# The two FFN layers of a streaming encoder: from plain tile products to Strassen's seven half-size products, with the hidden layer in three chunks

## The chip, the cores and the metric

One core of one Trainium2 chip runs the whole program in one launch. The metric is the device time of that launch in microseconds (us), as the median of several runs. Lower is better.

## What is computed

`x` is 512 tokens by 1024 features, float32. Two layers follow each other: an S5 state-space mixer and then a retention mixer, each followed by a SwiGLU FFN of width 2816, with an RMS norm ahead of each of the four and one at the end. The change touches the FFN alone:

```
def rmsnorm(x, g):
    y = x * lax.rsqrt(jnp.mean(jnp.square(x), axis=-1, keepdims=True) + 1e-6)
    return y * g
def swiglu(u, w_gate, w_up, w_down):                 # u: 512 x 1024
    h = jax.nn.silu(u @ w_gate) * (u @ w_up)         # w_gate, w_up: 1024 x 2816
    return h @ w_down                                # w_down: 2816 x 1024
x = x + swiglu(rmsnorm(x, ffn_norm[i]), ...)         # i = 0, 1
```

## The kernel before

Everything is kept transposed: features lie on the 128 partitions, the 512 tokens in the free dimension. `xT` is 8 such tiles, and the hidden layer is 22 (`FT`). Each float32 operand is split into a high part, rounded to the type float32r, and the remainder as a low part (`u_hi`, `u_lo`; `w_hi`, `w_lo`). `product` issues three matmuls for a 128 x 128 block of weights: high by high, high by low, low by high, each with 512 moving columns. The RMS norm's factor per token (`rs`) is applied to what comes out of the matmuls.

Weights arrive in units of up to 1 MB in two slots (`s` = 0 and 1). For each unit SyncE's queue loads `w_raw[s]`, ScalarE makes `w_hi[s]`, VectorE makes `w_lo[s]` by a subtraction (`split_weights`, once on each engine), and TensorE uses them; semaphores (`w_loaded`, `w_hi_ready`, `w_lo_ready`, `w_used`) count the pairs of units. Every engine runs its own instructions strictly in the order written; nothing is scheduled by a tool.

An FFN layer is a loop of 11 rounds. In a round, slot 0 holds 256 columns of the gate weights and slot 1 the same of the up weights, for two hidden tiles; each unit is 48 matmuls (2 tiles x 8 blocks x 3). VectorE takes the gate out of PSUM times `rs` (line 1544), ScalarE applies silu (line 1119), VectorE takes the up part out times `rs` and multiplies the two (line 1203), ScalarE makes `h_hi`, VectorE `h_lo` (line 1558). All 22 tiles of the hidden layer stay in SBUF. Then come the 8 output tiles: each is 22 blocks x 3 = 66 matmuls into one PSUM bank, and VectorE adds it to `xT` (line 1470), with the next norm's input and squares made right behind. A layer is 22 x 48 + 8 x 66 = 1584 matmuls of 512 columns.

Of the kernel before, what the change touches and what calls it, by code (L numbers as in the profile page):

```python
# [20 lines left out]

# [6 lines left out]
F32 = mybir.dt.float32  # L28
# [5 lines left out]
P = 128  # L34
# [23 lines left out]
PAIRS = {"glu": 2, "ffn0": 11, "down0": 8, "ret": 12, "wo": 4, "ffn1": 11, "down1": 8}  # L58
# [58 lines left out]
def bank_starts():  # L117
# [34 lines left out]
FREE0, FULL0 = bank_starts()  # L152

# [9 lines left out]
def trunk(nc, x, s5_norm, lam_re, lam_im, log_step, b_re, b_im, c_re, c_im, s5_d, glu_w, glu_b,  # L163
          ret_norm, ret_w, ret_gn, ret_wo, ffn_norm, ffn_gate, ffn_up, ffn_down, final_norm,
          ident_in, rope_in, decay_in, out):
    with ExitStack() as ctx:
# [105 lines left out]
        last.close()  # L272
        u_hi = sb(ctx, "u_hi", [P, KT, SEQ], F32R)
# [4 lines left out]
        y_whole = tmp[:, 6, :]  # L278
        sq = tmp[:, 4, :]
# [7 lines left out]
        ffn = ExitStack()  # L287
        h_hi = sb(ffn, "h_hi", [P, FT, SEQ], F32R)
        h_lo = sb(ffn, "h_lo", [P, FT, SEQ], F32R)
        ffn.close()  # L290
# [82 lines left out]
        w_used = [sem(f"w_used{s}") for s in range(2)]  # L373

# [43 lines left out]


# [28 lines left out]
        def _(sp):  # L448
# [62 lines left out]
            def ffn_units(layer):  # L511
                with sp.Fori(0, HT) as i:
                    load_unit(0, i + PAIR0[f"ffn{layer}"], gate_v[layer][:, :, bass.ds(i * 256, 256)], KT, 256)
                    load_unit(1, i + PAIR0[f"ffn{layer}"], up_v[layer][:, :, bass.ds(i * 256, 256)], KT, 256)
                with sp.Fori(0, KT) as i:
                    for s in range(2):
                        load_unit(s, i + PAIR0[f"down{layer}"],
                                  down_v[layer][:, HT * s:HT * s + HT, bass.ds(i * P, P)], HT, P)

            ffn_units(0)  # L520
# [15 lines left out]
            ffn_units(1)  # L536
# [8 lines left out]
        def _(pe):  # L545
# [222 lines left out]
            def rms_sum(norm):  # L768

                b0 = FREE0[f"norm{norm}"][7]  # L770
                pe.wait_ge(sum_done, (KT + 1) * (norm + 1))
                open_bank(7, b0)
                pe.matmul(bank[7][:, :], ones[:, :], sq_sum, start=True, stop=True).then_inc(bank_full[7], 1)
# [14 lines left out]
            def ffn_products(layer, norm):  # L788
                def hidden_tiles(i, s, split):

                    banks = [2 * s, 2 * s + 1]
                    two_tiles(s, i + PAIR0[f"ffn{layer}"], banks, [i + FREE0[f"ffn{layer}"][b] for b in banks],
                              split, KT * norm)

                hidden_tiles(0, 0, u_split)
                rms_sum(norm)
                hidden_tiles(0, 1, None)
                with pe.Fori(1, HT) as i:
                    for s in range(2):
                        hidden_tiles(i, s, None)  # L800
                with pe.Fori(0, KT // 2) as i:
                    for m in range(2):
                        b = 4 + m
                        open_bank(b, i + FREE0[f"down{layer}"][b])
                        for s in range(2):
                            pe.wait_ge(w_lo_ready[s], i * 2 + PAIR0[f"down{layer}"] + m + 1)
                            for k in range(HT):
                                kk = HT * s + k
                                pe.wait_ge(h_split, FT * layer + kk + 1)
                                mm = product(bank[b][:, :], s, slice(P * k, P * k + P), h_hi[:, kk, :],  # L810
                                             h_lo[:, kk, :], kk == 0, kk == FT - 1)
                            mm.then_inc(w_used[s], 1)

            ffn_products(0, 0)
# [75 lines left out]
            ffn_products(1, 2)  # L890
# [30 lines left out]
        def _(act):  # L921
# [150 lines left out]
            def root(i):  # L1072

                b = FULL0[f"norm{i}"][7]
                act.wait_ge(bank_full[7], b + 1)
                act.activation(rs, bank[7][:, :], ACT.Sqrt, bias=eps[:, :], scale=1.0 / D).then_inc(bank_free[7], 1)
# [5 lines left out]


            for t in range(KT):
# [7 lines left out]
                if t in GLU_SPLIT_AT:  # L1092
                    split_weights(m // 2, i + PAIR0["glu"] + 1)
                act.wait_ge(x_new, t + 1)
                u_high(0, t, V_FFN0)
                square(t)
            root(0)

            def ffn(layer, i_norm, gain_col):
                def body(i, last_of_all):  # L1100

                    for m in range(2):
                        pair = i * 2 + m + PAIR0[f"down{layer}"]
                        if not (last_of_all and m == 1):
                            split_weights(0, pair + 1)
                        if last_of_all and m == 1:
                            act.activation(small[:, 27:28], eps[:, :], ACT.Sqrt)
                        act.wait_ge(bank_free[4 + m], i + FREE0[f"down{layer}"][4 + m] + 1)
                        if i_norm < 3:
                            u_high(i_norm, i * 2 + m, gain_col)  # L1110
                        square(i * 2 + m)
                        if not (last_of_all and m == 1):
                            split_weights(1, pair + 1)

                with act.Fori(0, HT) as i:
                    pair = i + PAIR0[f"ffn{layer}"]
                    for m in range(2):
                        act.wait_ge(bank_free[m], i + FREE0[f"ffn{layer}"][m] + 1)
                        act.activation(sig[:, m, :], sig[:, m, :], ACT.Silu).then_inc(gate_ready, 1)  # L1119
                    split_weights(0, pair + 1)  # L1120
                    split_weights(1, pair + 1)
                    for m in range(2):
                        act.wait_ge(h_raw_ready, i * 2 + (FT * layer + m + 1))
                        copy(tile(h_hi, i * 2 + m), act_raw[:, m, :]).then_inc(h_hi_ready, 1)
                if layer == 0:
                    with act.Fori(0, KT // 2) as i:
                        body(i, False)
                else:
                    with act.Fori(0, KT // 2 - 1) as i:
                        body(i, False)  # L1130
                    body(KT // 2 - 1, True)

            ffn(0, 1, V_RET)
# [40 lines left out]
            with act.Fori(0, KT // 2) as i:  # L1174
                for s in range(2):
                    act.wait_ge(bank_free[2 + s], i + FREE0["wo"][2 + s] + 1)
                    u_high(2, i * 2 + s, V_FFN1)
                    square(i * 2 + s)
                    split_weights(s, i + PAIR0["wo"] + 1)
            root(2)  # L1180
            ffn(1, 3, V_FINAL)
# [9 lines left out]
        def _(dve):  # L1191
# [293 lines left out]
            def inverse_rms(i):  # L1485
                dve.wait_ge(bank_free[7], FREE0[f"norm{i}"][7] + 1)
# [7 lines left out]


# [20 lines left out]
            inverse_rms(0)  # L1516

            def ffn(layer, i_norm, gain_col):
                def body(i, last_of_all):

                    for m in range(2):
                        pair = i * 2 + m + PAIR0[f"down{layer}"]
                        if not (last_of_all and m == 1):
                            split_weights(0, pair + 1)
                        dve.wait_ge(w_used[1], pair + 1)
                        add_to_x(i * 2 + m, bank[4 + m][:, :]).then_inc(bank_free[4 + m], 1)
                        dve.wait_ge(bank_free[4 + m], i + (FREE0[f"down{layer}"][4 + m] + 1))
# [317 lines left out]
```

## Time and profile before

| | |
|---|---|
| median of 3 runs | 1275.46 us (1275.38 to 1276.29) |
| span of the profiled execution, first to last instruction | 1274.6 us |
| the times shown, less that span | 0.8 to 1.7 us |
| TensorE busy, of the span | 97% |
| VectorE, ScalarE, GpSimd busy | 53%, 36%, 5% |
| second FFN layer behind its norm's sum (1536 matmuls) | 348.2 us |

The profile gives no other time of the profiled execution than its span; what lies around it is the third row. Engines overlap, so the busy shares add up to more than one, and a share says nothing of which wait ends last. TensorE's rows come as matmuls (PE) and weight loads (PEld). The duration of a matmul's row reaches over the start of the next, so the pace of TensorE is read from starts.

### The profile page before, as it was taken

How to read it: one execution, taken by the hardware profiler on the slowest of the kernel's cores; microseconds unless marked ns; L12 is line 12 of the kernel's file. 1: busy time of each engine (PE TensorE's matmuls, PEld its weight loads, DVE VectorE, ACT ScalarE, POOL GpSimd, SP SyncE). 2: the span in 40 equal slices, each digit the busy share in tenths (PEclk: the TensorE clock that was granted, in tenths of full speed). 3: DMA queues.
4: the chain of work that ended last, by engine and by line, in shares of the span. 5: the costliest groups of instructions: out<-in, count | busy, mean ns of one | idle time of the engine just before them, and what ended most of it. 6: DMA issues, size and time to landing. Idle time of an engine off the chain costs nothing.

```text
span 1274.6 us, 16378 instructions
## 1 busy us (share of the span) xinstructions
PE 1240.5 (97%) x6469; PEld 1031.8 (81%) x6469; DVE 671.5 (53%) x771; ACT 463.7 (36%) x493; POOL 64.5 (5%) x84
## 2 busy tenths in 40 slices
PE   3899999999999999999999999999999999999997
PEld 3778888888888888888888888888888888888886
DVE  8997754443444444646655465643454444444443
ACT  6555443233333333333343333422333333332232
POOL 5940000000000000000000000000000000000000
PEclk9999999999999999999999999999999999999999
DMA  5663333333323334323232133233232323323331
GB/s 116 153 123 100 99 100 99 99 99 99 99 68 90 92 91 138 108 66 108 67 99 94 45 107 99 66 99 98 67 124 77 102 92 99 99 68 91 95 109 66
DMA packets 143376, 121.31 MB, mean 95 GB/s; under 512 B 5528, under 2 KB 135632, under 8 KB 143312
## 3 DMA queue, kind: packets, MB, share of 16 engines
q1 hardware_dynamic: 141680, 118.23, 30.3%
q10 hardware_dynamic: 1664, 2.62, 1.0%
q8 instruction: 23, 0.38, 0.1%
q14 instruction: 9, 0.07, 0.0%
HBM read 114.29 MB, written 2.10 MB: 91 GB/s over the span
## 4 chain that ended last, share of the span: by engine, by line
PE 93%; POOL 3%; DVE 1%; ACTq 1%; ACT 1%; DMA 0%; issue 0%; SPq 0%; DVEq 0%; POOLq 0%
PE bank L738 27%; PE bank L740 27%; PE bank L739 27%; PE bank L836 2%; PE bank L837 2%; PE bank L838 2%; ACTq L443 1%; PE bank L865 1%; PE bank L866 1%; PE bank L864 1%; PE bank L634 1%; PE bank L875 1%; POOL s_pool_tmp L1699 1%; POOL s_seg_tmp L1699 0%; ACT w_raw L929 0%; PE bank L849 0%
## 5 line engine op out<-in xcount | busy, mean ns | idle before, releaser
L738 PE MATMUL bank<-u_hi,w_hi 128*128 128x512 f32 x960 | 374.9, 390 | 0.0
L740 PE MATMUL bank<-u_hi,w_lo 128*128 128x512 f32 x960 | 373.6, 389 | 0.0
L739 PE MATMUL bank<-u_lo,w_hi 128*128 128x512 f32 x960 | 373.5, 389 | 0.0
L1213 DVE TENSOR_TENSOR w_lo<-w_raw,w_hi 128x2048 fp32r<-128x2048 f32 x112 | 256.5, 2291 | 167.0 <-ACT w_hi L929 166.9
L929 ACT ACTIVATE w_hi<-w_raw 128x2048 fp32r<-128x2048 f32 x112 | 214.0, 1911 | 318.3 <-PE bank L740 314.9
L738 PEld LDWEIGHTS bank<-u_hi,w_hi 128*128 128x128 f32 x960 | 180.2, 188 | 37.9 <-issue 0.6
L739 PEld LDWEIGHTS bank<-u_lo,w_hi 128*128 128x128 f32 x960 | 180.2, 188 | 37.5 <-issue 0.5
L740 PEld LDWEIGHTS bank<-u_hi,w_lo 128*128 128x128 f32 x960 | 180.2, 188 | 37.4
L738 PE MATMUL bank<-h_hi,w_hi 128*128 128x512 f32 x352 | 136.9, 389 | 0.0
L739 PE MATMUL bank<-h_lo,w_hi 128*128 128x512 f32 x352 | 136.9, 389 | 0.0
L740 PE MATMUL bank<-h_hi,w_lo 128*128 128x512 f32 x352 | 136.9, 389 | 0.0
L1203 DVE TENSOR_TENSOR tmp<-bank,tmp 128x512 f32<-128x512 f32 (+3 forms) x60 | 38.1, 635 | 97.0 <-PE bank L740 94.2
L1119 ACT ACTIVATE tmp<-tmp 128x512 f32<-128x512 f32 x44 | 27.8, 632 | 136.6 <-DVE tmp L1544 135.6
L1544 DVE TENSOR_TENSOR tmp<-bank,tmp 128x512 f32<-128x512 f32 x44 | 30.0, 691 | 89.7 <-PE bank L740 89.2
L740 PEld LDWEIGHTS bank<-h_hi,w_lo 128*128 128x128 f32 x352 | 66.1, 188 | 13.8
L739 PEld LDWEIGHTS bank<-h_lo,w_hi 128*128 128x128 f32 x352 | 66.1, 188 | 13.7
L738 PEld LDWEIGHTS bank<-h_hi,w_hi 128*128 128x128 f32 x352 | 66.1, 188 | 13.7
L1470 DVE TENSOR_TENSOR xT<-bank,xT 128x512 f32 (+1 forms) x24 | 16.6, 692 | 92.5 <-PE bank L740 92.5
L1069 ACT ACTIVATE u_hi<-xT,vecs (+1 forms) x24 | 17.3, 721 | 124.4 <-DVE xT L1470 124.4
L738 PE MATMUL bank<-y_hi,w_hi 128*128 128x512 f32 x128 | 49.9, 390 | 0.0
L739 PE MATMUL bank<-y_lo,w_hi 128*128 128x512 f32 x128 | 49.8, 389 | 0.0
L740 PE MATMUL bank<-y_hi,w_lo 128*128 128x512 f32 x128 | 49.8, 389 | 0.0
(230 smaller groups left out, 1320.1 us busy)
## 6 DMA issues: line engine op xcount, KB each, us to landing
w_raw<-in_ret_w_qkvg_dram SPq DMA_DIRECT2D x24, 1024.0 KB, 5.0
w_raw<-in_ffn_w_gate_dram SPq DMA_DIRECT2D x22, 1024.0 KB, 5.1
w_raw<-in_ffn_w_up_dram SPq DMA_DIRECT2D x22, 1024.0 KB, 5.1
w_raw<-in_ffn_w_down_dram SPq DMA_DIRECT2D x32, 704.0 KB, 4.2
w_raw<-in_ret_w_o_dram SPq DMA_DIRECT2D x8, 1024.0 KB, 5.1
w_raw<-in_s_glu_w_dram SPq DMA_DIRECT2D x4, 1024.0 KB, 4.8
s<-in_x_dram ACTq DMA_DIRECT2D x8, 256.0 KB, 7.9
s_w<-in_x_dram SPq DMA_DIRECT2D x1, 2048.0 KB, 8.9
```

Source lines behind the costliest of these rows:

```text
L738: pe.matmul(o, w_hi[w][:, w_cols], hi, start=first, stop=False)
L739: pe.matmul(o, w_hi[w][:, w_cols], lo, start=False, stop=False)
L740: return pe.matmul(o, w_lo[w][:, w_cols], hi, start=False, stop=end)
L836: pe.matmul(o, a_hi, w_hi[s][:, cols], start=(kk == 0), stop=False)
L837: pe.matmul(o, a_hi, w_lo[s][:, cols], start=False, stop=False)
L838: mm = pe.matmul(o, a_lo, w_hi[s][:, cols], start=False, stop=(kk == KT - 1))
L929: return act.activation(o, i, ACT.Copy, scale=scale)
L1069: act.activation(tile(u_hi, t), tile(xT, t), ACT.Copy, scale=vecs[:, bass.ds(t + gain_col, 1)]).then_inc(u_hi_ready, 1)
L1119: act.activation(sig[:, m, :], sig[:, m, :], ACT.Silu).then_inc(gate_ready, 1)
L1203: return dve.tensor_tensor(o, a, b, ALU.mult)
L1213: dve.tensor_tensor(w_lo[s][:, :], w_raw[:, s, :], w_hi[s][:, :].bitcast(F32), ALU.subtract).then_inc(w_lo_ready[s], 1)
L1544: dve.tensor_tensor(sig[:, m, :], bank[m][:, :], rs, ALU.mult).then_inc(bank_free[m], 1)
```

## The change

Where a hidden tile needs both its gate and its up product, the two are one block product: a 2 x 2 block of weights (up and gate; first and second half of the 1024 inputs) by a 2 x 2 block of `u` (halves of the inputs; halves of the tokens). Strassen's scheme (in Winograd's form) makes its four results of seven products of half blocks instead of eight. A unit of weights is now one hidden tile: 128 columns of up and 128 of gate, all 1024 inputs (`PART` = 512 elements is a quarter of it).

- `CHUNKS` cuts the 22 tiles into 8, 8 and 6. Behind each chunk come four down units (`D`), each 256 output columns by the chunk's tiles, added to `xT` at once. The first four tiles of a layer are plain (`C`, 48 matmuls of 512 columns each), the other 18 use seven products (`S`, 84 matmuls of 256 columns each). A layer has 34 units, all written out, with no loop.
- Four sums of the quarters of `u` (`s_raw`, then `s_hi`, `s_lo`) are made once a layer, one k (0 to 3) at a time, by `scaled_u`, `u_sums`, `u_sums_high` and `u_sums_low`, among the work of the units C2 and C3. `s_raw` lies in the place of `r_lo[0]`.
- Four sums of the quarters of the weights (`t_raw`) are made for every S unit by `sums`, split by `sum_high` and `sum_low`; three raw quarters are split by `raw_high` and `raw_low`.
- A partial result that two outputs share is copied by ScalarE from one PSUM bank into another (`seed`), on which TensorE goes on adding; the next product into the first bank waits for that copy (`seeded`). A fifth product is copied to SBUF (`p5_copy`) and added by VectorE (`up_out`).
- The up part isn't multiplied by `rs` any more; the output of each down unit is (`down_out`), with one more VectorE instruction for each of its two tiles.

```
-                with pe.Fori(1, HT) as i:
-                    for s in range(2):
-                        hidden_tiles(i, s, None)
+CHUNKS = [(0, 8), (8, 8), (16, 6)]
+PLAIN = 4
+DOWN = 4
...
+FACTORS_AT = {2: (0, 1), 3: (2, 3)}
...
+            def seven_unit(s, pair, n, unit):
+                x, y, z, w = 3 * s, 3 * s + 1, 3 * s + 2, 6 + s
+                seeds0 = 3 * (SEVENS[s] * layer + unit.z)
+                pe.wait_ge(w_lo_ready[s], pair + 1)
...
+                for k in range(KH):
+                    mm = terms(left(z), *raw(s, 1), k, *of_u(k, 0), k == 0, k == KH - 1)
+                mm.then_inc(z_ready[s], 1)
+                open_bank(w, wide_free(layer, n, s))
+                for k in range(KH):
+                    pe.wait_ge(s_split, KH * layer + k + 1)
+                    mm = terms(left(w), *summed(s, 1), k, *of_s(k, 0), k == 0, k == KH - 1)
+                mm.then_inc(p5_ready[s], 1)
+                pe.wait_ge(seeded[s], seeds0 + 1)
+                for k in range(KH):
+                    mm = terms(left(z), *summed(s, 2), k, *of_s(k, 1), False, k == KH - 1)
+                mm.then_inc(z_ready[s], 1)
+                for k in range(KH):
+                    terms(left(x), *raw(s, 2), k, *of_u(KH + k, 0), False, k == KH - 1)
+                pe.wait_ge(seeded[s], seeds0 + 2)
...
+            def down_unit(s, pair, n, unit):
...
+                if unit.j == 0:
+                    steps = [(m, k) for m in range(2) for k in range(tiles - 1)] + [(m, tiles - 1) for m in range(2)]
+                for m, k in steps:
+                    if k == 0:
+                        open_bank(6 + m, wide_free(layer, n, m))
...
+                        ks = FACTORS_AT[n]
+                        if FACTORS_AT.get(n - 1, ()):
+                            u_sums_low(layer, FACTORS_AT[n - 1][-1])
+                        if ks:
+                            u_sums(layer, ks[0])
+                        hidden(n - 1)
+                        if kind(n + 1) == "S":
+                            for k in ks[1:]:
+                                u_sums_low(layer, k - 1)
+                                u_sums(layer, k)
+                            u_sums_low(layer, KH - 1)
+                            prepare(n + 1)
+                            hidden_low(n - 1)
+                            continue
+                def down_out(n):
...
+                        mul(sig[:, m, :], bank[6 + m][:, :], rs).then_inc(bank_free[6 + m], 1)
+                        dve.wait_ge(bank_free[6 + m], wide_free(layer, n, m) + 1)
+                        add_to_x(2 * unit.j + m, sig[:, m, :]).then_inc(x_added, 1)
```

VectorE in the loop of before, one round of two hidden tiles (`tmp` holds the gate and up buffers; the register and wait instructions between are left out):

```order
L1544 TENSOR_TENSOR tmp<-bank,tmp 128x512 [waits bank_full0]
L1544 TENSOR_TENSOR tmp<-bank,tmp 128x512 [waits w_used0]
...
L1213 TENSOR_TENSOR w_lo<-w_raw,w_hi 128x2048 [waits w_hi_ready0]
...
L1203 TENSOR_TENSOR tmp<-bank,tmp 128x512 [waits bank_full2]
...
L1203 TENSOR_TENSOR tmp<-tmp 128x512 [waits gate_ready]
L1203 TENSOR_TENSOR tmp<-bank,tmp 128x512 [waits w_used1]
...
L1203 TENSOR_TENSOR tmp<-tmp 128x512 [waits gate_ready]
L1213 TENSOR_TENSOR w_lo<-w_raw,w_hi 128x2048 [waits w_hi_ready1]
...
L1558 TENSOR_TENSOR h_lo<-tmp,h_hi 128x512
```

The split of a slot's weights waits for one ScalarE instruction only (`w_hi_ready`).

VectorE in the change, from the last sum of `u` (k = 3, while or after C3 runs on TensorE) to the split of the weights for the first S unit, S4:

```order
L1799 TENSOR_TENSOR s_raw<-a_raw 128x256 [waits s_split,a_ready]
L1800 TENSOR_TENSOR s_raw<-a_raw,b_raw 128x256
L1802 TENSOR_TENSOR s_raw<-s_raw,a_raw 128x256 [waits dve_step]
L1804 TENSOR_TENSOR s_raw<-b_raw,s_raw 128x256 [waits dve_step]
L1808 TENSOR_TENSOR s_lo<-s_raw,s_hi 128x1024 [waits s_hi_ready]
L1820 TENSOR_TENSOR t_raw<-w_raw 128x1024 [waits w_loaded0,up_loaded0]
L1824 TENSOR_TENSOR t_raw<-w_raw,t_raw 128x512 [waits t_ready0]
L1826 TENSOR_TENSOR t_raw<-w_raw,t_raw 128x512 [waits dve_step]
L1833 TENSOR_TENSOR r_lo<-w_raw,r_hi 128x1536 [waits r_hi_ready0,s_split]
L1839 TENSOR_TENSOR w_lo<-t_raw,w_hi 128x2048 [waits w_hi_ready0]
```

One instruction of 2048 elements per slot has become a row of dependent ones, and the last of them is what TensorE's `w_lo_ready0` waits for.

ScalarE in the loop of before (one round, register instructions left out), and in the change one whole S unit (S6, in slot 0, while TensorE runs it; the rows of slot 1 prepare S7):

```order
L1119 ACTIVATE tmp<-tmp 128x512 [waits bank_free0]
L1119 ACTIVATE tmp<-tmp 128x512 [waits bank_free1]
...
L929 ACTIVATE w_hi<-w_raw 128x2048 [waits w_used0,w_loaded0]
L929 ACTIVATE w_hi<-w_raw 128x2048 [waits w_used1,w_loaded1]
...
L929 ACTIVATE h_hi<-tmp 128x512
...
L929 ACTIVATE h_hi<-tmp 128x512
```

```order
L1096 ACTIVATE r_hi<-w_raw 128x1536 [waits w_used1,up_loaded1,w_loaded1]
L1096 ACTIVATE bank<-bank 128x256 [waits bank_free0,z_ready0]
L1096 ACTIVATE hid_hi<-tmp 128x512 [waits h_raw_ready]
L1096 ACTIVATE w_hi<-t_raw 128x1024 [waits w_used1,t_ready1]
L1096 ACTIVATE tmp<-bank 128x256 [waits bank_free1,p5_ready0]
L1096 ACTIVATE bank<-bank 128x256 [waits bank_free1,z_ready0]
L1096 ACTIVATE w_hi<-t_raw 128x1024 [waits w_used1,t_ready1]
L1318 ACTIVATE tmp<-tmp 128x512 [waits bank_free3]
L1096 ACTIVATE bank<-bank 128x256 [waits bank_free0,z_ready0]
```

Between the two splits of the next unit's weights now stand the copies that TensorE waits for in the running unit.

## Rows read from the trace of the kernel before

**Rows 1.** The page: span, busy time, granted clock in tenths, chain that ended last.

```profile
span 1274.6 us, 16378 instructions
...
PE 1240.5 (97%) x6469; PEld 1031.8 (81%) x6469; DVE 671.5 (53%) x771; ACT 463.7 (36%) x493; POOL 64.5 (5%) x84
...
PEclk9999999999999999999999999999999999999999
...
PE 93%; POOL 3%; DVE 1%; ACTq 1%; ACT 1%; DMA 0%; issue 0%; SPq 0%; DVEq 0%; POOLq 0%
```

**Rows 2.** Stretches: us, then busy (count) of each engine, clock, DMA share, GB/s.

```profile
914.72:1262.93 348.21, 348.21 (x1539) 288.24 (x1538) 156.09 (x147) 114.27 (x101) 0.00 (x0) 1.00 0.28 87
```

**Rows 3.** Timeline, TensorE, the retention scores: start us, us, engine, line, operation.

```profile
551.07 0.28 PE L848 MATMUL bank<-y_hi,k_hi 128*128 128x256 f32 x1
...
551.78 0.22 PE L848 MATMUL bank<-y_hi,k_hi 128*128 128x128 f32 x1
551.84 0.28 PE L849 MATMUL bank<-qk_lo,k_hi 128*128 128x128 f32 x1
...
552.40 0.45 PE L738 MATMUL bank<-u_hi,w_hi 128*128 128x512 f32 x1
552.69 0.39 PE L739 MATMUL bank<-u_lo,w_hi 128*128 128x512 f32 x1
```

**Rows 4.** Timeline, VectorE, a round of the first FFN loop.

```profile
275.19 0.69 DVE L1203 TENSOR_TENSOR tmp<-tmp 128x512 f32<-128x512 f32 x1
275.80 0.68 DVE L1203 TENSOR_TENSOR tmp<-bank,tmp 128x512 f32<-128x512 f32 x1
...
277.21 2.29 DVE L1213 TENSOR_TENSOR w_lo<-w_raw,w_hi 128x2048 fp32r<-128x2048 f32 x1
279.42 1.29 DVE L1558 TENSOR_TENSOR h_lo<-tmp,h_hi 128x512 f32 x2
```

**Rows 5.** Timeline, VectorE: a dependent pair (84 us) and other sizes.

```profile
84.16 0.98 DVE L1441 TENSOR_TENSOR s_states<-s_states,s 128x784 f32<-128x784 f32 x1
85.17 0.98 DVE L1443 TENSOR_TENSOR s_states<-s_states,s 128x784 f32<-128x784 f32 x1
...
536.38 1.23 DVE L1614 TENSOR_TENSOR qk_lo<-qk,y_hi 128x1024 fp32r<-128x1024 f32 x1 [1.20 <-ACT y_hi L929]
537.52 1.22 DVE L1614 TENSOR_TENSOR qk_lo<-qk,k_hi 128x1024 fp32r<-128x1024 f32 x1
...
551.98 0.42 DVE L1203 TENSOR_TENSOR tmp<-bank,tmp 128x256 f32<-128x256 f32 x1 [0.15 <-PE bank L850]
```

**Rows 6.** Timeline, ScalarE, at the end of the GLU.

```profile
146.85 1.91 ACT L929 ACTIVATE w_hi<-w_raw 128x2048 fp32r<-128x2048 f32 x1
148.65 0.71 ACT L1069 ACTIVATE u_hi<-xT,vecs 128x512 fp32r<-128x512 f32 x1
149.26 0.62 ACT L1065 ACTIVATE tmp<-xT 128x512 f32<-128x512 f32 x1
```

**Rows 7.** Groups of instructions, shapes apart, ScalarE: busy us, mean ns, idle before.

```profile
L929 ACT ACTIVATE k_hi<-qk 128x1024 fp32r<-128x1024 f32 x4 | 4.2, 1043 | 0.0
```

**Rows 8.** Timeline, TensorE, ahead of and behind a pause.

```profile
53.08 0.37 PE L639 MATMUL bank<-s_d_diag,ident 16*16 16x16 f32 x16
55.94 0.29 PE L634 MATMUL bank<-s_tc,s_fb 64*16 64x128 f32 x2 [2.49 <-POOL s_tc L1805]
```

**Rows 9.** Stretches of 1 us behind that pause, columns as in rows 2.

```profile
56.00:57.00 1.00, 1.00 (x18) 0.88 (x20) 0.93 (x3) 0.00 (x0) 1.00 (x1) 0.87 1.17 152
57.00:58.00 1.00, 1.00 (x14) 0.71 (x12) 0.96 (x2) 0.00 (x0) 1.00 (x2) 0.50 0.94 114
...
60.00:61.00 1.00, 1.00 (x20) 0.85 (x18) 0.96 (x2) 0.36 (x1) 1.00 (x2) 0.93 0.92 101
```

**Rows 10.** Chain that ended last, in time: start, us, engine, line, count.

```profile
93.48 3.85 PE bank L686 x125
...
1262.93 0.79 PE bank L905 x8
```

**Rows 11.** DMA issues: destination, source, count, KB each, us to landing.

```profile
w_raw<-in_ret_w_o_dram SPq DMA_DIRECT2D x8, 1024.0 KB, 5.1
```

More of the change, by code:

```diff
@@ L152, with wide_free @@
 FREE0, FULL0 = bank_starts()
+NORM_BANK = [2, 7, 2, 7]
+FACTORS_AT = {2: (0, 1), 3: (2, 3)}
+def wide_free(layer, n, m):
+    before = sum(1 for i in range(n) if kind(i) == "D" or (kind(i) == "S" and i % 2 == m))
+    return FREE0[f"ffn{layer}"][6 + m] + before
 def repeated(ap, axis, n):
@@ new lines, in u_sums_high, with raw_high @@
+            def u_sums_high(layer, k):
+                act.wait_ge(s_raw_ready, KH * layer + k + 1)
+                copy(s_hi[:, k, :, :], s_raw[:, :, :]).then_inc(s_hi_ready, 1)
+            def raw_high(layer, n):
+                unit, s, pair = UNITS[n], n % 2, PAIR0[f"ffn{layer}"] + n // 2
+                act.wait_ge(w_loaded[s], (pair + 1) * 16)
+                act.wait_ge(up_loaded[s], (MADE[s] * layer + unit.q + 1) * 16)
+                act.wait_ge(w_used[s], pair if unit.j > 1 else pair - 2)
+                copy(r_hi[s][:, :], w_raw[:, s, PART:4 * PART]).then_inc(r_hi_ready[s], 1)
@@ L1096, in _ @@
                 square(t)
[L1097 to L1133, printed above, removed]
+            chunked_hidden(0, 0, V_FFN0, V_RET)
             root(1)
@@ new lines, in u_sums_low, with sums @@
+            def u_sums_low(layer, k):
+                dve.wait_ge(s_hi_ready, KH * layer + k + 1)
+                dve.tensor_tensor(s_lo[:, k, :, :], s_raw[:, :, :], s_hi[:, k, :, :].bitcast(F32),
+                                  ALU.subtract).then_inc(s_split, 1)
+            def sums(layer, n, half):
+                unit, s, pair = UNITS[n], n % 2, PAIR0[f"ffn{layer}"] + n // 2
+                raw = w_raw[:, s, :].rearrange("p (b a) -> p b a", b=4)
+                if half == 0:
+                    for before in [m for m in range(n) if kind(m) == "S"][-1:]:
+                        dve.wait_ge(w_lo_ready[before % 2], PAIR0[f"ffn{layer}"] + before // 2 + 1)
+                    dve.wait_ge(up_loaded[s], (MADE[s] * layer + unit.q + 1) * 16)
+                    dve.wait_ge(w_loaded[s], (pair + 1) * 16)
+                    dve.tensor_tensor(t_raw[:, 0:2, :], raw[:, 1::-1, :], raw[:, 0:3:2, :],
+                                      ALU.subtract).then_inc(t_ready[s], 1)
+                else:
+                    dve.wait_ge(t_ready[s], 2 * (SEVENS[s] * layer + unit.z) + 1)
+                    step(dve.tensor_tensor(t_raw[:, 2, :], raw[:, 1, :], t_raw[:, 1, :], ALU.subtract))
+                    settle()
+                    dve.tensor_tensor(t_raw[:, 3, :], raw[:, 3, :], t_raw[:, 2, :], ALU.subtract).then_inc(t_ready[s], 1)
@@ new lines, in raw_low, with sum_low @@
+            def raw_low(layer, n):
+                unit, s = UNITS[n], n % 2
+                dve.wait_ge(s_split, KH * (layer + 1))
+                dve.wait_ge(r_hi_ready[s], SEVENS[s] * layer + unit.z + 1)
+                dve.tensor_tensor(r_lo[s][:, :], w_raw[:, s, PART:4 * PART], r_hi[s][:, :].bitcast(F32), ALU.subtract)
+            def sum_low(layer, n):
+                s, pair = n % 2, PAIR0[f"ffn{layer}"] + n // 2
+                dve.wait_ge(w_hi_ready[s], pair + 1)
+                dve.tensor_tensor(w_lo[s][:, :], t_raw[:, :, :].rearrange("p b a -> p (b a)"), w_hi[s][:, :].bitcast(F32),
+                                  ALU.subtract).then_inc(w_lo_ready[s], 1)
```

560 lines of the change are left out of this document (452 added, 108 removed), and 8 rows, old and new, of tables (by_unit, fills).

## The prediction

> **What bounds the kernel now.** I read the page first: TensorE is busy 97% of the span, and 93% of the chain that ended last is TensorE; its clock is full in every slice [rows 1]. Then the stretch of the second FFN layer behind its norm's sum: 1536 matmuls in 348.21 us, TensorE busy all of it, VectorE 156 and ScalarE 114 us [rows 2]. So TensorE alone sets the time there, and one matmul of 512 columns costs 348.21 / 1536 = 0.2267 us, start to start. The other engines have room, but only as long as nobody gives them more to do than the time that TensorE leaves. The question is how fast TensorE runs half-width matmuls, and where VectorE and ScalarE can't keep up.
>
> **1. The matmuls.** An S unit has 84 matmuls of 256 columns where a tile had 48 of 512. Six of 256 stand in the scores: from the first one's start to the start of the next kind 0.71 us [rows 3], in each of the four heads, so 0.1183 each. A tile: 48 x 0.2267 = 10.88 us before, 84 x 0.1183 = 9.94 after; 36 tiles in two layers: 36 x 0.94 = **-33.9 us**. Plain tiles and down units have as many matmuls as before. Every nanosecond more per 256-column matmul costs 36 x 84 = 3.0 us, so this is the sensitive number. Below it lies the pace of the 128-column ones in the same rows, 0.112 (five from 551.84 to 552.40), above it 0.120 by the rounding of single starts.
>
> The Trainium skill ("TensorE: Matmul & The Clock Gate", back-to-back issue gap) gives N / 2.4 + 2.5 ns at full clock, 216 ns for 512 columns and 109 for 256. By it a tile would gain 10.37 - 9.17 = 1.2 us, the 36 of them 43. The trace has 227 and 118 here, and I go by the trace.
>
> **2. Prices for VectorE and ScalarE.** VectorE: 512 elements last 0.69, and the next independent instruction starts 0.61 after; 2048: 2.29 and 2.21 [rows 4]; 1024: 1.23 and 1.14; 256: 0.42, so 0.34 to the next; a dependent one starts 0.03 after the end [rows 5], I take 0.04, also between engines. 1536 lies between: 1.76 and 1.67. ScalarE: 2048 last 1.91, the next starts after 1.80; 512 with a factor 0.71 (0.61), without 0.62 (0.52) [rows 6]; 1024: 1.05 [rows 7] (0.95); 1536: 1.48 (1.38); 256 by the same slope 0.41.
>
> **3. Inside an S unit** (9.94 us). VectorE: `sums` 1.26 + 0.73 + 0.61, `gate_out`, `up_out`, `hidden_low`, `hidden` 0.61 each, `raw_low` 1.67, `sum_low` 2.21: 8.9 us, so it keeps up, but with 1 us to spare; if no instruction overlapped the next, 9.8. ScalarE: 1.38 + 4 x 0.41 + 2 x 0.95 + 2 x 0.55 = 6.0. TensorE's waits: the first 12 matmuls end at 1.58 (11 x 0.1183 + 0.28); ScalarE, behind `raw_high` (0.2 to 1.68), copies until 2.05; TensorE wants it at 24 x 0.1183 = 2.84. The second: ready 4.42, copied 4.87, wanted 5.68; the third: 7.3, 7.7, 8.52. `sum_low` can start at 6.0, when `sum_high` ends, and ends at 8.3. All hidden by 0.8 us or more: 0 us. If that cover were gone, each S unit would wait for what is missing, three times.
>
> **4. Ahead of the first S unit.** Here I laid out the whole chain, zero being C2's first matmul; C2 and C3 end at 2 x 10.88 = 21.8. VectorE's own work in it is 2 `gate_out`, 2 `hidden`, a `hidden_low` (5 x 0.61), the split for C3 (2.21), four `u_sums` of 1.7, four `u_sums_low` of 1.14, then for S4 `sums` 2.6, `raw_low` 1.67 and `sum_low` 2.29: 23.2 us, already more than 21.8. And the two engines take turns, since `s_raw` is one buffer and the order is fixed (end times):
> gate_out 0.9; silu and scaled_u(0) 2.8; u_sums(0) 4.6; hidden 5.2; hidden_high 5.8; plain_high for C3 7.6; its split 10.0 (in time for C3); hidden_low 10.6; u_sums_low(0) 11.7; u_sums(1) 13.4; gate_out 14.0; silu 14.7; u_sums_high(1) 15.7; scaled_u(2) 16.9; u_sums(2) 18.7; hidden 19.3; hidden_high 19.9; u_sums_high(2) 20.9; scaled_u(3) 22.1; u_sums(3) 23.9; u_sums_high(3) 25.0; u_sums_low(3) 26.2; sums for S4 28.8; raw_low 30.5; sum_low 32.7. Only then may TensorE begin S4: it stands 32.7 - 21.8 = 10.9 us, in both layers **+21.9 us**. The least is 1.5 us each (VectorE's work alone); I take the chain, since each step waits for a named semaphore. Late next is S5's split, but it ends about 9 us after S4 begins, in time.
>
> The pause costs the clock too. After the 2.5 us without matmuls at 53 to 56 us [rows 8] it was at half, 1.2 of 2.4 GHz, for three whole slices of 1 us and parts of two more: (0.13 + 3 x 0.5 + 0.07) / 0.5 = 3.4 us [rows 9]. At half clock half the work is done, so each pause costs 1.7 more: **+3.4 us** (0 to 5).
>
> **5. Down units.** In the first down unit of a chunk both output tiles end together, the first only 4 matmuls before the end (-0.91 + 0.39 = -0.52); the next unit opens the same bank, and VectorE empties it in 0.69, so TensorE waits 0.25; six times: **+1.5 us**. In the others the first tile ends half-way, and its bank is long empty. VectorE's work in a down unit: 4 x 0.65 + 2.21 (10.88 us of matmuls); in the last chunk, with the next norm's, 4 x 0.65 + 4 x 0.7 + 1.67 = 7.1 in a turn with ScalarE of about 7.5, against 36 x 0.2267 = 8.16: hidden. With `sums` and `raw_low` of the next chunk 9.1 of 10.88: hidden.
>
> **6. The end.** Before, TensorE went from the last FFN matmul straight on to the sums for the last norm [rows 10]. That sum needs tile 6's square added, and VectorE now does it behind both outputs: wait 0.2, two instructions for tile 7 (0.69 + 0.73), `final_gained` 0.5, the addition 0.65: **+2.7 us**.
>
> **7. Loads.** Pieces are 512 bytes now; the output projection of the retention has such pieces, 1 MB in 5.1 us [rows 11], and a slot is free 10 us ahead: 0. The program is written out instead of looped: TensorE has run 125 small matmuls of written-out code in 3.85 us [rows 10], 31 ns each, so reading the code shouldn't matter: 0 (what VectorE and ScalarE do in such code is in rows 5).
>
> **Sum.** -33.9 + 21.9 + 3.4 + 1.5 + 2.7 = -4.4 us on the profiled execution of 1274.6 us span; the median lies 0.9 above the span, and I add the change to it: 1275.5 - 4.4 = **1271.1 us**. So a good gain in 36 tiles is mostly given back in two pauses.
>
> **Rivals.**
> A. *As summed*: 1271.1, with +-2 us on the chain of step 4 twice and +-1.5 on the pace: 1267 to 1276. Chance 0.52.
> B. *Slower: the weight loads show at the waits.* An S unit has 8 waiting matmuls (the unit's start, four on `s_split`, three on `seeded`), A 256-column matmul leaves little beyond the load's 0.112. Where a unit starts behind short matmuls, 552.40 to 552.69 is 0.29, 0.06 more than the usual 0.23 [rows 3]. At 0.06 each it is 8 x 36 x 0.06 = 17 us, at a third 6: 1277 to 1288, middle 1283. It decides from 0.026 us per wait on (7 us) that the kernel is slower. Against it: the scores' first matmuls wait for their bank too and show nothing. Chance 0.18.
> C. *The pauses are short*: ScalarE and VectorE overlap better than I laid out, down to 1.5 us each, and the clock holds: 1271.1 - 18.8 - 3.4 = 1249. Speaks for it: nothing but an error of mine in the order. Chance 0.08.
> D. *The pauses are longer*, or VectorE's 1 us to spare in S units is used up after them (9.8 of 9.94, if it doesn't overlap): 3 us more per layer, 1277. Chance 0.13.
> E. *The matmuls run closer to the bare stream.* At the 0.112 of the 128-column rows, a tile is 9.41: 36 x 0.53 = 19 less, 1252. Chance 0.04. The page named in step 1 would have it at 1271.1 - 9 = 1262; that its figure for 512 columns misses this trace by 11 ns speaks against it.
> Something else, either way: 0.05.
>
> **Numbers.** Two runs of this kernel can tell 0.2% (2.6 us) from no change. Below 1272.9: most of A (0.36), C, E and a little: 0.49. Between 1272.9 and 1278: the rest of A, half of D, a little of B: 0.26. Above: 0.25. The range leaves out C and half of E below and the top of B above: 1262 to 1283.
>
> **What would show it.** Right: two idle stretches of TensorE of some 11 us ahead of the first 256-column matmuls, ended by VectorE's `w_lo` of 2048 elements, with a half clock behind them; 9.9 us per S unit, no waits for ScalarE's bank copies; VectorE near 90% busy in S stretches; some 2.7 us between the last FFN matmul and the last sums. Wrong: 256-column starts 0.12 or more apart, gaps at `seeded`, or pauses under 8 us.

## The result, and the profile after

| | before | after |
| --- | --- | --- |
| time, median (range) | 1275.70 us (1275.38 to 1276.29), 4 runs | 1281.92 us (1281.53 to 1282.37), 4 runs |
| ratio, 95% interval | | 1.0045 (1.0033 to 1.0057) |
| span of the profiled execution | 1274.6 us | 1279.9 us |

The changed kernel is slower by 0.45%, 6.2 us. A second comparison, on another chip, gave 1276.10 and 1281.29 us, ratio 1.0047 (1.0033 to 1.006). The forecast was 1271.1 us and a gain of 0.3%, so its sign was wrong; the range up to 1283 still holds the time.

The page after the change, to be read beside [rows 1]: TensorE is busy for less of the span and the clock is no longer full in every slice, although 1296 more matmuls are issued.

```profile
span 1279.9 us, 19023 instructions
...
PE 1221.5 (95%) x7765; PEld 1076.5 (84%) x7765; DVE 866.6 (68%) x1019; ACT 538.7 (42%) x705; POOL 64.1 (5%) x84
...
PEclk9999998999999999999999999999989999999999
...
PE 87%; DVE 5%; POOL 4%; ACT 1%; issue 1%; DMA 0%; ACTq 0%; DVEq 0%; SPq 0%; POOLq 0%
```

VectorE has come onto the chain with 5% of the span. Where, the chain in order of time says, in the second FFN layer (start, us, engine and tile, line): from one factor's `s_lo` to the next, and then through the first S unit's preparation, with no matmul between.

```profile
936.06 1.15 DVE s_lo L1808
941.23 1.24 DVE s_lo L1808
946.49 1.24 DVE s_lo L1808
951.77 1.23 DVE t_raw L1820
954.35 1.27 DVE r_lo L1833
956.02 2.29 DVE w_lo L1839
```

TensorE's waits after the change (what waited, for what: us in total, times, longest) have three lines in the FFN and behind it that the kernel before hasn't; `issue` is time in which the engine waited for nothing that the profile shows:

```profile
PE bank L876 <- DVE w_lo L1839: 21.7, 2, 10.9
...
PE bank L1072 <- DVE tmp L1764: 2.6, 1, 2.6
...
PE bank L821 <- issue: 0.9, 6, 0.2
```

**The pause.** TensorE's timeline ahead of the first S unit in layer 0: the last matmul of C3 starts at 187.75, the first of S4 at 199.01. Without a wait it would have started 0.23 later, at 187.98, so the pause costs 11.0 us; layer 1 has the same from 947.3 to 958.4.

```profile
187.75 0.39 PE L823 MATMUL bank<-u_hi,w_lo 128*128 128x512 f32 x1
199.01 0.58 PE L876 MATMUL bank<-u_hi,r_hi 128*128 128x256 f32 x1 [10.87 <-DVE w_lo L1839]
199.39 0.41 PE L877 MATMUL bank<-u_lo,r_hi 128*128 128x256 f32 x1
```

VectorE's timeline over the same stretch. It is hardly idle: the fourth factor's sums, `s_raw`, stand behind the third's split since they share a buffer; then ScalarE's turn for `s_hi`, and only then S4's own preparation, in the order in which step 4 had laid it out.

```profile
187.14 1.23 DVE L1808 TENSOR_TENSOR s_lo<-s_raw,s_hi 128x1024 fp32r<-128x1024 f32 x1 [1.65 <-ACT s_hi L1096]
188.47 0.42 DVE L1799 TENSOR_TENSOR s_raw<-a_raw 128x256 f32<-128x256 f32 x1
...
189.72 0.42 DVE L1804 TENSOR_TENSOR s_raw<-b_raw,s_raw 128x256 f32<-128x256 f32 x1
191.27 1.23 DVE L1808 TENSOR_TENSOR s_lo<-s_raw,s_hi 128x1024 fp32r<-128x1024 f32 x1 [1.12 <-ACT s_hi L1096]
192.41 1.22 DVE L1820 TENSOR_TENSOR t_raw<-w_raw 128x1024 f32<-128x1024 f32 x1
...
195.00 1.75 DVE L1833 TENSOR_TENSOR r_lo<-w_raw,r_hi 128x1536 fp32r<-128x1536 f32 x1
196.67 2.28 DVE L1839 TENSOR_TENSOR w_lo<-t_raw,w_hi 128x2048 fp32r<-128x2048 f32 x1
```

**The clock behind it.** Stretches, columns as in [rows 2] (us; busy and count of TensorE, its weight loads, VectorE, ScalarE, GpSimd; granted clock; DMA share; GB/s). The clock falls to one half, 1.2 GHz, inside the pause, and stays there until 202.5 in layer 0 and until 963.7 in layer 1.

```profile
188.00:199.00 11.00, 0.13 (x1) 0.00 (x0) 9.64 (x12) 6.25 (x6) 0.00 (x0) 0.70 0.00 0
199.00:200.00 1.00, 0.99 (x4) 0.99 (x5) 1.00 (x2) 0.00 (x0) 0.00 (x0) 0.50 0.00 0
...
202.00:203.00 1.00, 1.00 (x8) 1.00 (x8) 1.00 (x3) 1.00 (x2) 0.00 (x0) 0.73 1.15 348
...
963.00:964.00 1.00, 1.00 (x7) 1.00 (x7) 0.76 (x1) 0.11 (x1) 0.00 (x0) 0.64 0.01 4
1267.00:1268.00 1.00, 1.00 (x9) 1.00 (x10) 0.00 (x0) 0.05 (x1) 0.00 (x0) 0.75 0.00 0
1268.00:1269.00 1.00, 1.00 (x6) 1.00 (x6) 0.00 (x0) 0.00 (x0) 0.00 (x0) 0.50 0.00 0
```

**The pace of the 256-column matmuls**, TensorE's timeline inside an S unit: 0.12 from start to start over whole units, wherever the clock is full.

```profile
309.78 0.28 PE L876 MATMUL bank<-u_hi,r_hi 128*128 128x256 f32 x1
309.90 0.28 PE L877 MATMUL bank<-u_lo,r_hi 128*128 128x256 f32 x1
```

**The end.** TensorE's timeline: the last FFN matmul starts at 1263.36, the sums for the last norm at 1266.38, 3.0 later where the kernel before has 0.2; and 16 small transposes, of which the kernel before does 16 in 1.95 us (its timeline: `1263.58 1.95`, L899), now take 3.46, since the clock is at one half, as the last two stretches above show.

```profile
1263.36 0.39 PE L823 MATMUL bank<-hid_hi,w_lo 128*128 128x512 f32 x1
1266.38 1.05 PE L1072 MATMUL bank<-ones,tmp 128*128 128x1 f32 x8 [2.63 <-DVE tmp L1764]
1267.29 3.46 PE L1066 MATMUL bank<-ident,final 128*128 128x128 f32 x16
```

The account of the span, each term from the rows above or from the same views elsewhere:

| term | us | from |
| --- | --- | --- |
| 36 tiles, 84 x 0.1200 = 10.08 instead of 10.88 | -28.9 | start-to-start times |
| two pauses | +22.1 | 187.98 to 199.01, 947.3 to 958.36 |
| half clock behind them | +4.1 | 16 matmuls in 3.57 (from 199.01) and 25 in 5.45 (from 958.36) instead of 0.12 each |
| openings of down units (the first matmul into a bank that VectorE has just emptied) | +2.8 | six of 0.39, two of 0.22 |
| not assigned, up to the last FFN matmul | +0.7 | it starts at 1263.36, before at 1262.54; 0.2 of it lies ahead of the first FFN matmul, at 143.55 and before at 143.36 |
| wait ahead of the last sums | +2.8 | 3.02 instead of 0.23 |
| half clock in the last transposes and sums | +1.7 | 3.46 instead of 1.95, and the rows behind |
| sum | +5.3 | span: +5.3 |

The rest up to the medians' 6.2 us lies outside the span: the time was 1.8 to 3.6 us above the span in the nine runs of this kernel, 1.73 to 1.84 in those of the kernel before in the comparisons below.

### The profile page after: what moved, and what is told of

Its sections match the earlier page's. It is cut to its first block, busy times and chain, and to the rows that moved or that the text cites. A ratio compares the mean times of both kernels' runs of the same rounds, so it can differ in the third digit from the quotient of the medians.

```text
span 1279.9 us, 19023 instructions
## 1 busy us (share of the span) xinstructions
PE 1221.5 (95%) x7765; PEld 1076.5 (84%) x7765; DVE 866.6 (68%) x1019; ACT 538.7 (42%) x705; POOL 64.1 (5%) x84
## 4 chain that ended last, share of the span: by engine, by line
PE 87%; DVE 5%; POOL 4%; ACT 1%; issue 1%; DMA 0%; ACTq 0%; DVEq 0%; SPq 0%; POOLq 0%
PE bank L821 16%; PE bank L823 15%; PE bank L822 15%; PE bank L876 10%; PE bank L878 10%; PE bank L877 10%; PE bank L1004 2%; PE bank L1005 2%; PE bank L1003 2%; POOL s_pool_tmp L2151 1%; POOL s_seg_tmp L2151 1%; PE bank L1033 1%; PE bank L1032 1%; PE bank L1031 1%; POOL s_tc L2256 1%
## 5 line engine op out<-in xcount | busy, mean ns | idle before, releaser
L1096 ACT ACTIVATE w_hi<-w_raw 128x2048 fp32r<-128x2048 f32 (+1 forms) x68 | 126.6, 1862 | 172.4 <-PE bank L823 153.6
L821 PE MATMUL bank<-u_hi,w_hi 128*128 128x512 f32 x448 | 175.7, 392 | 0.0
L823 PE MATMUL bank<-u_hi,w_lo 128*128 128x512 f32 x448 | 174.4, 389 | 0.0
L822 PE MATMUL bank<-u_lo,w_hi 128*128 128x512 f32 x448 | 174.3, 389 | 0.0
L1510 DVE TENSOR_TENSOR w_lo<-w_raw,w_hi 128x2048 fp32r<-128x2048 f32 x44 | 100.8, 2290 | 55.2 <-ACT w_hi L1096 55.1
L876 PE MATMUL bank<-s_hi,w_hi 128*128 128x256 f32 x432 | 123.0, 285 | 0.0
L878 PE MATMUL bank<-s_hi,w_lo 128*128 128x256 f32 x432 | 122.9, 285 | 0.0
L877 PE MATMUL bank<-s_lo,w_hi 128*128 128x256 f32 x432 | 122.9, 285 | 0.0
L821 PE MATMUL bank<-hid_hi,w_hi 128*128 128x512 f32 x288 | 113.0, 392 | 0.9 <-issue 0.9
L822 PE MATMUL bank<-hid_lo,w_hi 128*128 128x512 f32 x288 | 112.2, 389 | 0.0
```

The source lines that it names most:

```text
L821: pe.matmul(o, w_hi[w][:, w_cols], hi, start=first, stop=False)
L822: pe.matmul(o, w_hi[w][:, w_cols], lo, start=False, stop=False)
L823: return pe.matmul(o, w_lo[w][:, w_cols], hi, start=False, stop=end)
L876: pe.matmul(o, wh[:, cols], hi, start=first, stop=False, skip_group_check=True)
L877: pe.matmul(o, wh[:, cols], lo, start=False, stop=False, skip_group_check=True)
L878: return pe.matmul(o, wl[:, cols], hi, start=False, stop=end, skip_group_check=True)
```

## The experiments

### One part alone: half-width matmuls in the old kernel

`pace256` is the kernel before with the 512 columns of the second layer's gate and up products done as two parts of 256, `pace192` the same with 192 and 320. No other engine's work changes.

```diff
+            def in_parts(b, s, cols, hi, lo, k, first, end):
+                for p0, p1 in ((0, 256), (256, 512)):
+                    o, wide = bank[b][:, p0:p1], slice(p0, p1)
+                    pe.matmul(o, w_hi[s][:, cols], hi[:, k, wide], start=first, stop=False, skip_group_check=True)
+                    pe.matmul(o, w_hi[s][:, cols], lo[:, k, wide], start=False, stop=False, skip_group_check=True)
+                    mm = pe.matmul(o, w_lo[s][:, cols], hi[:, k, wide], start=False, stop=end, skip_group_check=True)
```

In both, the second layer's hidden values aren't the reference's; where the expectation of `pace256` says otherwise, it is mistaken. The matmuls, their sizes and their order are as it says, and only these are read here.

> The kernel before, with every gate and up matmul of the second FFN layer cut into two of 256 columns (same weights loaded twice, same banks, nothing else changed); the result is the same. Theory 1: 0.120 us from start to start is what a long stream of 256-column matmuls costs, whatever surrounds it; then the 22 tiles cost 96 x 0.120 = 11.52 instead of 10.88 us each, +14.0 us, about 1290, and nearly all starts lie 0.12 apart. Theory 2: a stream runs at the 0.1183 of the scores, and the other 1.7 ns come from what the seven-product units do around their matmuls (copies between banks, waits, two sets of weights); then +10.5 us, about 1286, and one start in five lies 0.11 or the mean is 0.118.

Measured: 1289.60 us, span 1287.8. That is 13.5 above the 1276.08 us of the kernel before in the same comparison (15 runs), 0.5 short of theory 1's 14.0 and 3.0 above theory 2; it is one run. What decides is its timeline: it shows the pace directly, 0.120 each, with the same interval through the whole stretch:

```profile
999.83 0.28 PE L749 MATMUL bank<-u_lo,w_hi 128*128 128x256 f32 x1
999.95 0.28 PE L750 MATMUL bank<-u_hi,w_lo 128*128 128x256 f32 x1
```

So the pace has nothing to do with S units, their waits or the engines beside them.

> As the last, but cut into 192 and 320 columns. If the weight load is the floor of a half-size matmul, the step behind a 192-column matmul stays at 0.11 to 0.12 us although only 192 columns stream; the 320-column one takes 0.147 (320 at 2.4 GHz and the 13 ns that a 512-column one has on top); 48 x 0.267 = 12.8 us a tile, +42 us, about 1318. If the columns set the pace, the step is 0.09 and a tile 11.5 us, +13 us, about 1289.

Measured: 1309.43 us, 33.4 above, between the two forecasts. Neither theory holds as it stood: behind the three matmuls of 192 columns the next start comes after 0.09, 0.11 and 0.12, behind those of 320 after 0.15 on the mean; the six together take 0.777.

```profile
1000.60 0.25 PE L748 MATMUL bank<-u_hi,w_hi 128*128 128x192 f32 x1
1000.69 0.27 PE L749 MATMUL bank<-u_lo,w_hi 128*128 128x192 f32 x1
1000.80 0.28 PE L750 MATMUL bank<-u_hi,w_lo 128*128 128x192 f32 x1
```

The weight loads of the same stretch stand at 1000.60, 1000.71, 1000.83 and 1000.94: there is one for each matmul, and where the matmuls are short the loads follow each other every 0.11 to 0.12. That the loads hold the short matmuls back fits this, and the 0.112 of the 128-column matmuls [rows 3]; no run takes the loads away to show it.

```profile
1000.71 0.19 PEld L750 LDWEIGHTS bank<-u_hi,w_lo 128*128 128x128 f32 x1
1000.83 0.19 PEld L748 LDWEIGHTS bank<-u_hi,w_hi 128*128 128x128 f32 x1
```

If it is so, 256 columns at 0.120 lie just above the floor, and pieces much smaller than these would gain nothing more.

### One cost taken away: the pauses

`early6` keeps the Strassen units but gives six tiles to the plain way instead of four, and spreads the sums over the four units from C1 on: one factor in each of C1 to C4, behind the next unit's split instead of ahead of it. VectorE's part of the diff (ScalarE's is alike):

```diff
-PLAIN = 4
+PLAIN = 6
-FACTORS_AT = {2: (0, 1), 3: (2, 3)}
+SUM_AT = {1: 0, 2: 1, 3: 2, 4: 3}
...
+                        if kind(n + 1) != "S":
+                            prepare(n + 1)
+                        u_sums_low(layer, SUM_AT[n - 1])
+                        if n in SUM_AT:
+                            u_sums(layer, SUM_AT[n])
                         hidden(n - 1)
                         if kind(n + 1) == "S":
-                            for k in ks[1:]:
-                                u_sums_low(layer, k - 1)
-                                u_sums(layer, k)
-                            u_sums_low(layer, KH - 1)
                             prepare(n + 1)
-                            hidden_low(n - 1)
-                            continue
```

> The changed kernel with six plain tiles instead of four, one sum of u in each of the units C1 to C4, and the split of the next plain unit's weights ahead of it. Theory: VectorE and ScalarE have the sums done before the first seven-product unit; both pauses (2 x 11.0) and the half clock behind them (4.2 us) go, the four more plain tiles cost 4 x (10.88 - 10.08) = 3.2 us: -23.0, about 1259. A pause of up to 1 us may stay. Rival: the pauses are not what the chain of sums costs but move elsewhere (S units wait instead): no faster than 1275.

Measured: 1259.82 us (1258.37 to 1261.02), ratio 0.9867 (0.9851 to 0.9882). Beside the change's own ratio that is 0.0178, 22.7 us, for 23.0 expected. TensorE's timeline at the start of the first S unit (VectorE's has `w_lo` from 207.41, 2.29 long, so it ends at 209.70): the first 256-column matmul follows the last of 512 after 0.23.

```profile
209.52 0.39 PE L823 MATMUL bank<-u_hi,w_lo 128*128 128x512 f32 x1
209.75 0.39 PE L876 MATMUL bank<-u_hi,r_hi 128*128 128x256 f32 x1
209.97 0.28 PE L877 MATMUL bank<-u_lo,r_hi 128*128 128x256 f32 x1
```

The line `w_lo` is gone from TensorE's waits in both layers, and the clock stays full there. This settles that the two pauses, with the clock behind them, made the kernel slower: with them gone the same units make it 1.3% faster. Whether the two more plain tiles or the spread sums alone would have done it isn't separated. It also shows how little room is left: 0.05 us.

The end of this trace shows something else. The wait ahead of the last sums is the changed kernel's, 2.63 us, but the half clock begins inside it and lasts until 10.0 us behind the restart; in the changed kernel it lasted 3.4 in all. Both groups of transposes are slow, and the part from the last FFN matmul to the end of the span takes 18.6 us instead of 16.5.

```profile
1250.26 3.53 PE L1066 MATMUL bank<-ident,final 128*128 128x128 f32 x16
```

### One cost taken away: the end

`tail` has VectorE finish tile 6 with its square before it turns to tile 7.

```diff
-                down_out(len(UNITS) - 1)
-                next_norm(len(UNITS) - 1)
+                for m in range(2):
+                    down_out(len(UNITS) - 1, (m,))
+                    next_norm(len(UNITS) - 1, (m,))
```

> The changed kernel, with the last down unit's two output tiles taken out one after the other, each with its norm work right behind (in both layers), as the kernel before did. Theory: the 2.8 us in which TensorE waits for tile 6's square at the end goes away, and with it the half clock behind that pause (1.8 us): -4.5 us, 1277.4. Rival: the half clock at the end comes from elsewhere and stays: -2.7 us, 1279.2.

Measured: 1277.95 us (1277.25 to 1280.92, 11 runs), ratio 1.0013 (1.0004 to 1.0022); beside the change's ratio 0.0032, 4.1 us, for 4.5 expected. TensorE's timeline: the wait is 0.9 us instead of 2.6, and the 16 transposes take 1.94 us again.

```profile
1267.15 1.02 PE L1072 MATMUL bank<-ones,tmp 128*128 128x1 f32 x8 [0.88 <-DVE tmp L1500]
1268.04 1.94 PE L1066 MATMUL bank<-ident,final 128*128 128x128 f32 x16
```

This execution reached its first FFN matmul 2.3 us later than the changed kernel's (145.82 and 143.55), so the two traces are compared from the last FFN matmul on. From there to the end of the span it takes 13.1 us instead of 16.5: 1.8 less ahead of the sums, 1.7 less behind them, where the clock now stays full. The 3.4 together lie within what the medians' 4.1 leaves open (some 2 us either way, by the intervals of the two ratios).

### One cost taken away: the openings of the down units

`first_down` lets the first output tile of a chunk's first down unit end earlier, so that VectorE has emptied its bank when the next unit opens it. The last `k` of `h_split`, for which the old order waited, keeps its place near the end.

```diff
-                        steps = [(m, k) for m in range(2) for k in range(tiles - 1)] + [(m, tiles - 1) for m in range(2)]
+                        steps = [(0, k) for k in range(tiles - 1)] + [(1, k) for k in range(3)]
+                        steps += [(0, tiles - 1)] + [(1, k) for k in range(3, tiles)]
```

> The changed kernel with one other order of the blocks in the first down unit of each chunk: the first output tile gets its last block behind three blocks of the second tile, so that it ends half-way and its PSUM bank is empty when the next unit opens it. Theory: the six gaps of 0.39 us (0.54 and 0.31 in place of 0.23) at the start of the second down unit go: -2.3 us, 1279.5 beside 1281.9. Rival: the next bank or VectorE's load of work takes their place: same as the changed kernel within 0.5.

`after_again` is the changed kernel as it is, measured on the same chip as `first_down`:

> The changed kernel as it is, once more, beside the versions made from it on the same chip. The first comparison gave 1281.9, of which the span accounts for 5.3 of the 6.2 us above the kernel before. If the longer written-out program costs time ahead of or behind its span, the time lies 2.5 us above the span again (1.75 for the others); if that was chance, the difference is 1.75 as for the others and the median about 1281.5.

Measured: 1279.02 us (1278.34 to 1280.33, 10 runs) beside 1281.29 (1280.55 to 1284.17, 5 runs): 2.3 us less, as expected. The timelines of the two kernels at the same place, the changed one first, then `first_down`: the gap of 0.54 with its `issue` is an ordinary 0.23 again, and so it is at all six places. The times of `after_again` lie 2.0 to 3.6 us above their spans (median 2.1), those of the kernel before 1.8: the extra outside the span comes again, smaller than the 2.5 of the expectation.

```profile
251.65 0.39 PE L823 MATMUL bank<-u_hi,w_lo 128*128 128x512 f32 x1
252.19 0.47 PE L821 MATMUL bank<-hid_hi,w_hi 128*128 128x512 f32 x1 [0.15 <-issue]
252.50 0.39 PE L822 MATMUL bank<-hid_lo,w_hi 128*128 128x512 f32 x1
```

```profile
251.17 0.39 PE L823 MATMUL bank<-u_hi,w_lo 128*128 128x512 f32 x1
251.40 0.39 PE L821 MATMUL bank<-hid_hi,w_hi 128*128 128x512 f32 x1
```

### One cover taken away: the copies between banks

`seed_late` puts ScalarE's first bank copy of an S unit behind two other instructions.

```diff
-                        seed(n, 1)
                         if kind(n - 1) == "S" and kind(n - 2) in ("C", "S"):
                             hidden_high(n - 2)
                         if kind(n + 1) == "S":
                             sum_high(layer, n + 1, 0)
+                        seed(n, 1)
```

> The changed kernel with ScalarE's first bank copy of an S unit put behind the two instructions that followed it (the high part of a hidden tile and the first half of the next weights' sums). It tests that the copies are hidden with some 0.8 us to spare. By the trace the copy ends 0.83 us before TensorE wants it; 1.55 us later it is 0.75 late: where both instructions are there (10 units a layer) 0.75 each, where only one is (5) about 0.2: +17 us, about 1299, with gaps ahead of the third group of matmuls ended by ScalarE. Rival: there is more room than that (TensorE's matmuls before the wait are enough): no change.

Measured: 1298.62 us (one run), 17.3 above `after_again`. In the changed kernel ScalarE's timeline has this copy at 212.41, and it ends 0.8 ahead of the matmul that wants it at 213.61; here it starts at 213.11, TensorE stands, and its next two matmuls come slowly. There are 20 such waits.

```profile
PE bank L876 <- ACT bank L1096: 10.4, 20, 0.5
```

```profile
212.74 0.28 PE L878 MATMUL bank<-s_hi,w_lo 128*128 128x256 f32 x1
213.53 0.39 PE L876 MATMUL bank<-s_hi,w_hi 128*128 128x256 f32 x1 [0.51 <-ACT bank L1096]
213.75 0.28 PE L877 MATMUL bank<-s_lo,w_hi 128*128 128x256 f32 x1
```

Two matmuls that should start 0.12 apart start 0.79 apart, and the one behind 0.22: 0.77 us lost for a wait listed with 0.5, 15.4 of the 17.3 us. Eight units that have only one of the two instructions behind show a shorter gap, 0.26 to 0.28 and again 0.22 behind it: 0.25 us each, 2.0 in all. Both sizes are as expected. So the zero of step 3 was a zero by cover, which the changed kernel has.

### All three mends together

`best` is `early6`, `tail` and `first_down` in one.

> All three mends in one: six plain tiles with the sums of u spread over C1 to C4 (measured 22.7 us faster than the change), the last down unit's tiles one after the other (4.1), the other order in the first down units (2.3 expected). If they add up: 1281.9 - 29.1 = 1252.8, 1.8% faster than the kernel before. Rival: one mend uncovers what another hid, and 2 us or more of it are lost.

Measured: 1252.75 us (1251.86 to 1253.64), ratio to the kernel before 0.9817 (0.9803 to 0.983), so 23.4 us faster than it and 28.5 faster than the change: the three mends add up as expected. Its page and its waits: TensorE 97% busy, and no wait in the FFN layers at all; a stretch from 514 to 1235 us is busy to the last hundredth.

```profile
PE 1214.7 (97%) x7621; PEld 1065.5 (85%) x7621; DVE 848.2 (68%) x999; ACT 527.3 (42%) x681; POOL 64.3 (5%) x84
```

```profile
514.00:1235.00 721.00, 721.00 (x3872) 626.46 (x3872) 450.22 (x504) 278.46 (x321) 0.00 (x0) 1.00 0.29 91
```

## Why the prediction was wrong, by its own steps

**Step 1 failed in size, and this is the largest miss: -28.9 us instead of -33.9.** "256-column starts 0.12 or more apart" was the first sign of being wrong that the prediction names, and it came. The mechanism was right; the term was 0.1183 us per 256-column matmul, and it measured 0.1200, in the changed kernel and in `pace256` alone. I took it from the quotient of a run of six [rows 3], and put 0.120 down to the rounding of single starts. Rounding it was not: all four heads show the same 0.71, so those six take 0.118 each. But they are a short run between matmuls of other widths, and at such edges the distances are odd (551.78 to 551.84 is 0.06, the next are 0.112 [rows 3]); why a short run is quicker no run here shows. The trace had a better source: the long stretch of [rows 2] gives 226.7 ns for 512 columns, and 512 columns at 2.4 GHz are 213.3, so 13.3 ns on top; 256 columns with the same 13.3 are 120.0, as measured. The Trainium skill ("TensorE: Matmul & The Clock Gate", back-to-back issue gap) puts 2.5 ns on top, by which 256 columns would be 109 ns, and calls this the gap of an isolated matmul; in the stream of `pace256` it is 120. Rival E, which went that way, is out. The first 5.0 of 10.8 us between forecast and time are these.

**Step 4's chain was right**: a pause of 11.0 us in each layer (10.9 forecast), at the named place, ended by `w_lo`. It was right link by link: with zero at 166.2, C2's first matmul, it puts the end of the last `u_sums_low` at 192.4, of `sums` at 195.0, of `raw_low` at 196.7 and of `sum_low` at 198.9, and VectorE's timeline shows 192.50, 195.08, 196.75 and 198.95. Rivals C (short pauses) and D (longer pauses, 3 us more per layer) are out. Its clock term was low: 3.4 forecast, 4.1 measured, 1.65 in layer 0 and 2.45 in layer 1, since the half clock lasted 3.6 us from the restart in one and 5.4 in the other. But that size is not the kernel's: behind the same pause it lasted 3.7 and 5.5 us in `after_again`, 6.2 and 3.5 in `tail`, 3.1 and 3.1 in `first_down`. If 44% of that time is lost, as 0.120 instead of 0.213 makes it, these are by estimate 2.7 to 4.2 us for two pauses, and 3.4 lies among them. `early6` confirms the sum of both from the other side.

**Steps 2 and 3 held.** ScalarE's copy of 256 took 0.37 us (0.41 forecast), `r_hi` 1.49, VectorE's 1536 elements 1.75, and no matmul waited for a copy. VectorE was busy for 35.6 of the 40 us from 310 on and for 28.8 of those from 1090 on, 89% and 72% for 90% forecast. Rival B, weight loads that show at each wait, is out: the matmuls that wait in an S unit start in the common 0.12, and where they really have to wait, in `seed_late`, the restart costs 0.10 at the second matmul. The measured time lies inside B's band, 1277 to 1288, but by other terms; that is chance.

**Step 5 was low**, 2.8 for 1.5. Six openings cost 0.39 instead of 0.25, because the matmul behind the opening comes late too (0.31 for 0.227); and two later ones, not named in it, cost 0.22 each. `first_down` took 2.3 us away.

**Step 6 had the wait right and its consequence missing.** The wait was 2.8 us for 2.7, by the four instructions that it names. But I had priced the clock behind the pauses of step 4 and not behind this one: +1.7 us. I had read in [rows 8, 9] that a pause of 2.5 us is followed by half clock, and this one has 2.6. `tail` shows both parts. The size is again that of an execution: with the same wait, the half clock ended 4.5 to 4.7 us behind the restart in three traces, 8.7 in `seed_late` and 10.0 in `early6`.

**Step 7 held**: no wait in the FFN layers is for a transfer.

Nothing in the forecast stands for the last 1.8 us: 0.7 inside the span that I can't assign, and 1.1 between how the profiled execution and the median stand after the change and before. Of the latter, some 0.3 to 0.7 us is longer time outside the span, which the changed kernel and `first_down` show by their medians, `seed_late` with 0.9 in its one run, `tail` with under 0.2, and `early6` and `best`, with as much code, not at all. Its cause stays open.

The misses are 5.0, 0.2, 0.7, 1.3, 0.1, 1.7 and 1.8, together the 10.8 us between 1271.1 and 1281.9. They all have one sign. The forecast gain was 4.4 us, the difference of terms of 34 and 30 us: an error of 5 us in the largest was enough to turn it.

## What to carry to other kernels

When one engine is to get cheaper units from work that others must prepare, lay out the others' chain up to the first such unit, and start it as many units earlier as it is long; here two more plain tiles per layer, with the sums spread over four units, cost some 3.2 us of gain and saved 26. Take the price of a smaller instruction from the longest uniform stretch of the larger one, split into the part that scales and the part that doesn't, and check it against the short run, not the other way round. Price the clock behind every pause of an engine that was busy up to it, the one at the program's end too.

## What was unexpected of the hardware

- A matmul with its own weight load costs the same 13.3 ns on top of its columns at 2.4 GHz in two sizes: 226.7 ns for 512 and 120.0 for 256. At half clock that is gone: 0.213 between starts for 256 columns, just the columns at 1.2 GHz (201.73 to 202.37 in the changed kernel: three intervals in 0.64). Half clock thus costs 44% of the time that 256-column matmuls spend in it, not 50%.
- Short matmuls with a load each come no closer than about 0.11 us on the mean: three of 192 columns took 0.32 us together, 0.107 each, where 192 columns and 13.3 ns would be 0.093. That the loads do it is a reading of their rows, not shown by a run.
- Pauses of one and the same length, 11.0 us, were followed by 3.1 to 6.2 us of half clock, from one layer to the other and from one execution to the next. The wait of 2.6 us at the end was followed by 3.4 us of it in the changed kernel, beginning 1.1 us behind the restart, and by 10.0 us in `early6`; the one of 0.9 us in `tail` and `best` by none.
- After a wait of 0.5 us the second matmul comes 0.10 late as well, so a wait costs more than its line says.
